# Two attention stages: cross attention's head order and output unit, local attention's scores, minimum and products

## The chip, the cores and the metric

The kernel runs on one core of one Trainium2 chip. The metric is the device time of one launch in microseconds (us). TensorE (PE) multiplies, VectorE (DVE) and ScalarE (ACT) do the elementwise work and empty PSUM, SyncE (SP) issues the weight loads. The engines run their own instruction streams in order and meet through semaphores.

## The reference

Two blocks of a small language model follow each other, 512 tokens wide 1024, all in float32. The first has two layers of mixer, memory cross attention and gated MLP; the second a gated linear attention layer and a local attention layer, each with an MLP. The two parts that matter here:

```python
def memory_cross_attention(x, mem_n, w_q, w_k, w_v, w_o):     # twice; 4 heads of 256, 256 memory rows
    s = einsum('bshd,bmhd->bhsm', q, k) * (256 ** -0.5)
    p = softmax(s, axis=-1)
    o = einsum('bhsm,bmhd->bshd', p, v).reshape(B, S, D_MODEL)
    return o @ w_o
```

The local attention (once) has 16 query heads of 64, two key heads, blocks of 128 queries that see their own and the previous block, a relative position bias with a mask in it, and one learned sink logit for each head, which enters the softmax's maximum and sum but has no value:

```
s = q k / 8 + bias[h];   m = max(max_k s, sink[h]);   p = exp(s - m) / (sum_k exp(s - m) + exp(sink[h] - m));   o = p v
```

## The kernel before

Activations lie with features on the partitions: `xs` is 8 tiles of 128 features by 512 tokens. A weight matrix comes in units of 128 x 2048 numbers. SP loads a unit into one of two raw buffers, ACT rounds it into `w_hi` (`split_hi`, L1206), DVE subtracts to get `w_lo` (`split_lo`, L1704), and a product with it is three matmuls (`mm3`: high by high, high by low, low by high), so that a unit of 256 output features is 8 tiles x 2 halves x 3 = 48 matmuls of 512 columns. The activations are split the same way (`high` on ACT, `rest` on DVE, into `xh` and `xl`). The products inside attention (queries by keys, transposes, probabilities by values) are plain float32, and PE runs each as two instructions.

All of PE's results go to eight PSUM banks. `plan_banks` (L120) lists the fills of every bank in PE's order; `wait_full`, `wait_free` and `wait_drained` wait for a fill, for the bank to be empty before a fill, and for the fill to have been read out. The order of work is the order written in each engine's program; there is no scheduler.

Cross attention is a pipeline of steps over the four heads. In step h PE computes the scores of head h (`s`), the output `o` of head h-2, and transposes the probabilities of head h-1 (`pT`). ACT takes the exponentials of head h straight from PSUM with a row sum, DVE finds the row maximum (L2048) before that and multiplies by the reciprocal of the sum afterwards (L2041, signal `p_ready`); both engines share the copies of `pT`; ACT and DVE split the output of a head into `xh` and `xl`. `queries_ahead` weaves the first two steps between the four query units: unit 0, unit 1, step 0, unit 2, step 1, unit 3, steps 2 to 5. On DVE the call before step 1 is `split_lo` of the output unit 0, which waits for ACT's half of that unit (`w_hi`), and ACT can't make that before query unit 2 is used up. After step 5 PE runs the four output units `xo`; unit 0 waits tile by tile for the heads' outputs.

Local attention (`swa`) runs 16 items, each a pair of heads (j = 0, 1, in partitions 0 to 63 and 64 to 127 of a query tile) by half of the sequence (nn: two blocks, n = 0, 1). In step `it` PE computes the scores of item `it`, half a half unit of the next queries (12 matmuls, up to step 11), the outputs of item it-2 and the transposes of item it-1; in the last steps it takes tiles of the output unit `so` in between. Scores of head j contract 64 rows; outputs of head j go to 64 columns of the array, that is to partitions 64j to 64j+63 of one bank. DVE adds the bias while reading PSUM (L2338, L2339, L2344), reduces the sum to the row maximum (L2341, L2342, L2347), takes the maximum with the sink and negates it (L2349, signal `rowmax_ready`); ACT takes the exponentials in place (L1665); DVE normalises (L2328, `p_ready`); PE transposes (L1158); ACT drains the transposes into `spT`. The even items (nn = 0) have three quarters of the columns, as the first block has no previous one. On ACT the drains of item it-2 stand ahead of the exponentials of item it, and behind those of item it-1.

Of the kernel before, what the change touches and what calls it, by code (L numbers as in the profile page):

```python
# [24 lines left out]
ACT = mybir.ActivationFunctionType  # L25
# [94 lines left out]
def plan_banks():  # L120
# [133 lines left out]
    for l in range(2):  # L254
# [8 lines left out]
        pairs(f"xo{l}", 4)  # L263
# [123 lines left out]
def build(nc, x, mem, params, consts, table, w_gk2, sinks, w, out):  # L387
    scratch = nc.dram_tensor("rel_scratch", [16, 384], F32, kind="Internal").ap()
    with ExitStack() as ctx:
# [41 lines left out]
        sb(ctx, "row_pad", [P, 120])  # L431
# [204 lines left out]
        def _(pe):  # L636
# [217 lines left out]

            def cross_attention(l):
# [3 lines left out]
                def step(h):  # L859
# [11 lines left out]
                    if h >= 2:  # L871
                        g = h - 2
                        if l == 1 and g == 0:
                            wait_drained(pe, ("mv1b", 1, 1))
                        for mt in range(MT):
                            wait_drained(pe, (name, "pT", g, mt))
# [129 lines left out]
            for l in range(2):  # L1006
# [3 lines left out]
                for j in range(4):  # L1010
                    feature_unit(f"xo{l}", j, ready=(lambda k: wait_drained(pe, (f"xa{l}", "o", k // 2, k % 2))) if j == 0 else None)
# [96 lines left out]
            def swa(it):  # L1108
# [4 lines left out]
                if it < SWA_ITEMS:  # L1113
                    hp, nn = it // 2, it % 2
                    if nn == 0:
                        wait_drained(pe, ("sq", hp // 2, hp % 2))
                    for j in range(2):
                        key = ("swa", "s", it, j)
                        wait_free(pe, key)
                        r = slice(64 * j, 64 * j + 64)  # L1120
                        for n in range(2):
                            blk = 2 * nn + n
                            lo = max(blk - 1, 0) * P
                            wd = (blk + 1) * P - lo
                            last = mm(bank(key)[:, (n + 1) * 256 - wd:(n + 1) * 256], qv[r, hp, blk * P:(blk + 1) * P],
                                      kk[r, hp // 4, lo:lo + wd], True, True)
                        full(last, key)
                if it in SWA_QUERIES:
                    half_unit("sq", 1 + it // 4, it // 2 % 2, range(4 * (it % 2), 4 * (it % 2) + 4), xtile)
                if it >= 2:  # L1130
# [5 lines left out]
                    for j in range(2):  # L1136
                        wait_drained(pe, ("swa", "pT", g, j))
                        for n in range(2):
                            blk = 2 * nn + n
# [53 lines left out]
        def _(act):  # L1193
# [435 lines left out]
            def drain_bias(m):  # L1629
                key = ("bias", m)  # L1630
                drain(key, bias[:, 2 * m:2 * m + 2, :], bank(key)[:, :].rearrange("p (h k) -> p h k", h=2))
# [20 lines left out]
            def swa(it):  # L1652
# [5 lines left out]
                if it < SWA_ITEMS:  # L1658
                    hp, nn = it // 2, it % 2
                    for j in range(2):  # L1660
                        seen.next("rowmax_ready")
                        for n in range(2):
                            lo = P if 2 * nn + n == 0 else 0
                            s_ = mh[:, it % 2, j, n * 256 + lo:(n + 1) * 256]
                            act.activation(s_, s_, ACT.Exp, bias=rmax[:, it % 2, 2 * j + n:2 * j + n + 1],  # L1665
# [24 lines left out]
        def _(dve):  # L1690
# [325 lines left out]
            def queries_ahead(split, drain_unit, step, steps):  # L2016
                for j in range(4):
                    split(j)
                    if j >= 2:
                        step(j - 2)  # L2020
                    drain_unit(j)
                for s in range(2, steps):
                    step(s)

            def cross_attention(l):
                name = f"xa{l}"

                def step(h):
# [4 lines left out]
                    if 1 <= h <= HEADS:  # L2033
# [8 lines left out]
                        give(last, "p_ready")  # L2042
                    if h < HEADS:
# [263 lines left out]
            def scaled_queries(j, m):  # L2307
                key = ("sq", j, m)
                wait_full(dve, key)
                free(dve.scalar_tensor_tensor(qv[:, 2 * j + m, :], bank(key)[:, :], 0.125, rstd[:, :], ALU.mult, ALU.mult), key)  # L2310
# [159 lines left out]
```

## Time and profile before

| | us |
|---|---|
| median of 3 runs | 2598.83 (2593.54 to 2599.11) |
| the profiled execution | 2598.96 |
| its span, first to last instruction | 2597.2 |
| PE busy in the span | 2488.3 (96%) |
| DVE busy | 1504.2 (58%) |
| ACT busy | 881.0 (34%) |

All times below are in us from the start of the span. Cross attention of layer 0 lies at about 330 to 402, of layer 1 at about 920 to 993; local attention runs from 2089 to 2190. 1.8 us of the profiled execution's time lie outside its span.

### The profile page before, as it was taken

What the parts mean: (1) busy time and instruction counts of PE and PEld (TensorE: products, weight loads), DVE (VectorE), ACT (ScalarE), POOL (GpSimd) and SP (SyncE); (2) the same over time, 40 slices, a digit from 0 to 9 for tenths busy, and PEclk for the clock granted to TensorE, in tenths of its full rate; (3) what the DMA queues carried; (4) which work ended last, traced back from release to release, by engine and by line L of the source; (5) the groups of instructions that cost most, each with busy time, mean ns of one, the idle gap of its engine ahead of it and who ended that gap; (6) DMA issues with size and microseconds to landing.
All of it is one profiled execution on the core that took longest, in us unless ns stands there. A gap on an engine that the chain in (4) does not pass through costs nothing.

```text
span 2597.2 us, 29768 instructions
## 1 busy us (share of the span) xinstructions
PE 2488.3 (96%) x11776; PEld 2036.6 (78%) x11776; DVE 1504.2 (58%) x2043; ACT 881.0 (34%) x1184; POOL 9.9 (0%) x23
## 2 busy tenths in 40 slices
PE   8999999999999799999998999999999998999998
PEld 7898777788887577788886788778888777788886
DVE  6887634644446834644446535556666686566666
ACT  3444533422223543422224434322222455322222
POOL 0000000000000000000000000000000000000000
PEclk9998999999999799999999999999999999999999
DMA  5222211322222121222222220132222211222221
GB/s 187 81 82 85 94 65 65 103 95 96 96 97 94 53 79 65 77 95 95 95 96 82 81 98 33 67 116 96 96 97 97 81 49 49 81 97 97 97 97 65
DMA packets 32816, 225.56 MB, mean 87 GB/s; under 512 B 3766, under 2 KB 3814, under 8 KB 6369
## 3 DMA queue, kind: packets, MB, share of 16 engines
q1 hardware_dynamic: 31536, 220.21, 24.7%
q0 software_dynamic: 1200, 4.23, 0.4%
q8 instruction: 57, 0.93, 0.1%
q14 instruction: 23, 0.18, 0.0%
HBM read 222.30 MB, written 2.12 MB: 86 GB/s over the span
## 4 chain that ended last, share of the span: by engine, by line
PE 83%; DVE 10%; ACT 4%; issue 2%; DMA 0%; DVEq 0%; SPq 0%; ACTq 0%
PE bank L640 83%; DVE w_lo L1708 2%; ACT w_hi L1207 1%; ACT xs L1266 1%; DVE xs L1791 1%; ACT xh L1220 1%; DVE cacc L1899 1%; DVE hs L1950 0%; DVE xs L1805 0%; DVE xs L1760 0%; DVE xl L1716 0%; DVE gs L1950 0%; DVE mh L2328 0%; DVE rmax L2347 0%; DVE mh L2344 0%
## 5 line engine op out<-in xcount | busy, mean ns | idle before, releaser
L640 PE MATMUL bank<-xh,w_hi 128*128 128x512 f32 x1976 | 789.7, 400 | 59.1 <-DVE xl L1716 22.0
L640 PE MATMUL bank<-xl,w_hi 128*128 128x512 f32 x1976 | 779.3, 394 | 0.0
L640 PE MATMUL bank<-xh,w_lo 128*128 128x512 f32 x1976 | 778.3, 394 | 0.0
L1708 DVE TENSOR_TENSOR w_lo<-w_raw,w_hi 128x2048 fp32r<-128x2048 f32 x205 | 469.6, 2291 | 410.3 <-ACT w_hi L1207 409.8
L1207 ACT ACTIVATE w_hi<-w_raw 128x2048 fp32r<-128x2048 f32 x205 | 391.2, 1909 | 373.2 <-PE bank L640 373.1
L640 PEld LDWEIGHTS bank<-xh,w_hi 128*128 128x128 f32 x1976 | 377.0, 191 | 158.9 <-issue 36.6
L640 PEld LDWEIGHTS bank<-xh,w_lo 128*128 128x128 f32 x1976 | 377.0, 191 | 80.2
L640 PEld LDWEIGHTS bank<-xl,w_hi 128*128 128x128 f32 x1976 | 377.4, 191 | 79.2 <-issue 2.2
L1760 DVE TENSOR_TENSOR xs<-xs,bank 128x512 f32<-128x512 f32 x448 | 294.2, 683 | 116.6 <-PE bank L640 115.4
L640 PE MATMUL bank<-mhh,w_lo 128*128 128x512 f32 x512 | 199.2, 389 | 0.0
L640 PE MATMUL bank<-mhh,w_hi 128*128 128x512 f32 x512 | 199.2, 389 | 0.0
L640 PE MATMUL bank<-mhl,w_hi 128*128 128x512 f32 x512 | 199.2, 389 | 0.0
L1851 DVE TENSOR_TENSOR mh<-bank,rstd 128x512 f32<-128x512 f32 x64 | 43.9, 692 | 178.6 <-PE bank L640 178.6
L1331 ACT ACTIVATE mhh<-mh 128x512 fp32r<-128x512 f32 x64 | 39.5, 633 | 317.3 <-DVE mh L1856 317.3
L640 PE MATMUL bank<-fhh,w_hi 128*128 128x512 f32 x352 | 136.9, 389 | 0.0
L640 PE MATMUL bank<-fhl,w_hi 128*128 128x512 f32 x352 | 136.9, 389 | 0.0
L640 PE MATMUL bank<-fhh,w_lo 128*128 128x512 f32 x352 | 136.9, 389 | 0.0
L1226 ACT ACTIVATE sq<-xs 128x512 f32<-128x512 f32 x88 | 54.7, 630 | 185.3 <-DVE xs L1760 69.4
L640 PEld LDWEIGHTS bank<-mhl,w_hi 128*128 128x128 f32 x512 | 96.1, 188 | 20.1
L640 PEld LDWEIGHTS bank<-mhh,w_hi 128*128 128x128 f32 x512 | 96.1, 188 | 19.9
L640 PEld LDWEIGHTS bank<-mhh,w_lo 128*128 128x128 f32 x512 | 96.1, 188 | 19.8
L1849 DVE TENSOR_TENSOR fh<-sil,bank 128x512 f32<-128x512 f32 x44 | 30.0, 687 | 116.6 <-PE bank L640 109.5
(286 smaller groups left out, 2719.9 us busy)
## 6 DMA issues: line engine op xcount, KB each, us to landing
w_raw<-weights_in SPq DMA_DIRECT2D x205, 1024.0 KB, 4.9
xs<-x_in SPq DMA_DIRECT2D x4, 512.0 KB, 8.0
sf<-rel_scratch POOLq DMA_DIRECT2D x1, 2048.0 KB, 11.8
y_out<-xs SPq DMA_DIRECT2D x8, 256.0 KB, 2.0
w_raw<-weights_in SPq DMA_DIRECT2D x2, 512.0 KB, 6.8
mk<-mem_in POOLq DMA_DIRECT2D x1, 1024.0 KB, 8.7
sum_q<-consts_in POOLq DMA_DIRECT2D x1, 256.0 KB, 8.9
scan<-consts_in POOLq DMA_DIRECT2D x1, 256.0 KB, 2.9
```

Of the source, the lines that this page charges most:

```text
L640: return pe.matmul(dst, a, b, start=start, stop=stop)
L1207: act.activation(w_hi[:, c % 2, :], w_raw[:, c % 2, :], ACT.Copy).then_inc(w_hi_ready, 1)
L1220: give(act.activation((xh if dst is None else dst)[:, k, :], src, ACT.Copy, **kw), "x_hi")
L1226: give(act.activation(sq[:, k % 2, :], src, ACT.Square), "sq_ready")
L1266: give(act.activation(xs[:, k, :], xs[:, k, :], ACT.Identity, scale=col(f"{param}_g{l}", k), bias=col(f"{param}_b{l}", k)), "xn_ready")
L1331: give(act.activation(hh[:, chunk % 2, m, :], src, ACT.Copy), "hh_ready")
L1708: dve.tensor_tensor(w_lo[:, c % 2, :], w_raw[:, c % 2, :], w_hi[:, c % 2, :].bitcast(F32), ALU.subtract)\
L1760: free(dve.tensor_tensor(xs[:, k, :], xs[:, k, :], bank(key)[:, :], ALU.add), key)
L1791: centred[k] = steps.step(dve.tensor_tensor(x_at(k), x_at(k), mean[:, :], ALU.subtract))
L1849: free(dve.tensor_tensor(hid[:, m, :], sil[:, m, :], bank(key)[:, :], ALU.mult), key)
L1851: free(dve.tensor_tensor(hid[:, chunk % 2, m, :], bank(key)[:, :], rstd[:, :], ALU.mult), key)
L1899: ins = dve.scalar_tensor_tensor(a, u, wj, a, ALU.mult, ALU.add)
```

## The change

In the plan of banks and on PE, the output unit 0 of cross attention moves to banks 4 and 5, which the scores have left, and its tiles are issued in pairs: tiles 0 and 1 in step 4 ahead of the outputs of head 2, tiles 2 and 3 in step 5 ahead of the outputs of head 3, tiles 4 to 7 after step 5.

```diff
         queries_ahead(f"xq{l}", cross(f"xa{l}"), HEADS + 2)
-        pairs(f"xo{l}", 4)
+        fill((f"xo{l}", 0, 0), 4)
+        fill((f"xo{l}", 0, 1), 5, UNITS[f"xo{l}"])
+        for j in range(1, 4):
+            pair(f"xo{l}", j)
...
+            def out_tiles(l, tiles):
+
+                stage = f"xo{l}"
+                c = UNITS[stage]
+                if tiles[0] == 0:
+                    pe.wait_ge(w_lo_ready, c + 1)
+                    for m in range(2):
+                        wait_free(pe, (stage, 0, m))
+                for k in tiles:
+                    wait_drained(pe, (f"xa{l}", "o", k // 2, k % 2))
+                    for m in range(2):
+                        last = mm3(bank((stage, 0, m))[:, :], weights(c, k * 256 + m * P, P), xtile(k), k == 0, k == KT - 1)
+                        if k == KT - 1:
+                            full(last, (stage, 0, m))
...
                         g = h - 2
                         if l == 1 and g == 0:
                             wait_drained(pe, ("mv1b", 1, 1))
+                        if h >= HEADS:
+                            out_tiles(l, range(2 * (h - HEADS), 2 * (h - HEADS) + 2))
...
                 queries_ahead(f"xq{l}", cross_attention(l), HEADS + 2, tile_ready)
-                for j in range(4):
-                    feature_unit(f"xo{l}", j, ready=(lambda k: wait_drained(pe, (f"xa{l}", "o", k // 2, k % 2))) if j == 0 else None)
+                out_tiles(l, range(4, KT))
+                for j in range(1, 4):
+                    feature_unit(f"xo{l}", j)
```

On DVE the normalisation of head 0 in step 1 moves ahead of the split of the output unit 0; the split of query unit 3 stays at the head of step 0.

```diff
-                def step(h):
+                def step(h, unit=None):
...
                         give(last, "p_ready")
+                    if unit is not None:
+                        split_lo(unit)
                     if h < HEADS:
...
-                queries_ahead(lambda j: j and split_lo(UNITS[f"xq{l}"] + j + 1), lambda j: None, cross_attention(l), HEADS + 3)
+                step = cross_attention(l)
+                split_lo(UNITS[f"xq{l}"] + 2)
+                for h in range(HEADS + 3):
+                    step(h, UNITS[f"xq{l}"] + 3 + h if h < 2 else None)
```

In local attention the score is kept negated: queries are scaled by -0.125, the bias is drained with scale -1, the sinks are negated once into `nskb`, and one DVE instruction for each block adds the bias and reduces to the minimum, seeded with the negated sink. It replaces the additions, the reductions and the small instruction behind them. ACT's exponential gets scale -1, and waits for the bank to be drained in place of `rowmax_ready`.

```diff
+            steps.step(dve.tensor_scalar(nskb[:, :], skb[:, :], -1.0, None, ALU.mult))
+            steps.wait()
...
-                        s_ = mh[:, it % 2, j, :]
-                        m_ = rmax[:, it % 2, 2 * j:2 * j + 2]
                         wait_full(dve, key)
-                        if nn == 0:
-                            dve.tensor_tensor(s_[:, P:2 * P], bank(key)[:, P:2 * P], bias[:, h, P:2 * P], ALU.add)
-                            free(dve.tensor_tensor(s_[:, 2 * P:], bank(key)[:, 2 * P:], bias[:, h, :], ALU.add), key)
-                            wait_drained(dve, key)
-                            dve.reduce_max(m_[:, 0:1], s_[:, P:2 * P], AX.X)
-                            steps.step(dve.reduce_max(m_[:, 1:2], s_[:, 2 * P:], AX.X))
-                        else:
-                            free(dve.tensor_tensor(s_.rearrange("p (n k) -> p n k", n=2), bank(key)[:, :].rearrange("p (n k) -> p n k", n=2),
-                                                   bias[:, h, :].unsqueeze(1).broadcast_to([P, 2, 2 * P]), ALU.add), key)
-                            wait_drained(dve, key)
-                            steps.step(dve.reduce_max(m_, s_.rearrange("p (n k) -> p n k", n=2), AX.X))
-                        steps.wait()
-                        give(dve.tensor_scalar(m_, m_, skb[:, h:h + 1], -1.0, ALU.max, ALU.mult), "rowmax_ready")
+                        for n in range(2):
+                            lo = P if 2 * nn + n == 0 else 0
+                            a = slice(n * 256 + lo, (n + 1) * 256)
+                            last = dve.tensor_tensor_reduce(mh[:, it % 2, j, a], bank(key)[:, a], bias[:, h, lo:], 1.0, nskb[:, h:h + 1],
+                                                            ALU.add, ALU.min, rmax[:, it % 2, 2 * j + n:2 * j + n + 1])
+                        free(last, key)
```

On PE the loops over heads and blocks are exchanged: both heads' banks (scores) or both heads' drained transposes (outputs) are waited for first, and then the products of the two heads alternate.

```diff
                     for j in range(2):
                         wait_drained(pe, ("swa", "pT", g, j))
-                        for n in range(2):
-                            blk = 2 * nn + n
-                            for kt in range(2):
-                                if blk + kt == 0:
-                                    continue
-                                v = (blk - 1 + kt) * P + (hp // 4) * 64
+                    for n in range(2):
+                        blk = 2 * nn + n
+                        for kt in range(2):
+                            if blk + kt == 0:
+                                continue
+                            v = (blk - 1 + kt) * P + (hp // 4) * 64
+                            for j in range(2):
                                 last = mm(bank(key)[64 * j:64 * j + 64, blk * P:(blk + 1) * P], vt[:, v:v + 64],
```

## Rows read from the trace of the kernel before

**Rows 1.** The page, part 1: engine, busy us, share, instructions.

```profile
PE 2488.3 (96%) x11776; PEld 2036.6 (78%) x11776; DVE 1504.2 (58%) x2043; ACT 881.0 (34%) x1184; POOL 9.9 (0%) x23
```

**Rows 2.** PE's waits, 357 to 413 (layer 0): total us, times, longest.

```profile
PE bank L891 <- DVE pr L2041: 2.6, 1, 2.6
PE bank L640 <- ACT pT L1212: 1.7, 2, 0.8
```

**Rows 3.** Timeline of PE, layer 1: start, length, [idle before].

```profile
953.51 1.38 PE L891 MATMUL bank<-ident,pr 128*128 128x128 f32 x8 [2.62 <-DVE pr L2041]
```

**Rows 4.** Stretch of steps 0 to 11: length, busy of each engine, PE clock.

```profile
2088.60:2160.00 71.40, 70.11 (x459) 53.13 (x460) 66.91 (x203) 45.37 (x148) 0.00 (x0) 1.00 0.13 45
```

**Rows 5.** Waits of PE 2088.6 to 2160; of PE, then ACT, 2160 to 2190.

```profile
PE bank L640 <- DVE sf L2310: 1.1, 2, 0.6
...
PE bank L640 <- ACT spT L1212: 6.1, 4, 2.9
...
ACT mh L1665 <- DVE rmax L2349: 7.3, 8, 1.8
```

**Rows 6.** Two stretches of low clock; the columns as in rows 4.

```profile
363.75:367.16 3.41, 3.41 (x13) 3.02 (x12) 2.03 (x6) 1.93 (x8) 0.00 (x0) 0.51 0.69 274
...
2183.05:2186.47 3.42, 3.42 (x19) 2.99 (x15) 2.00 (x2) 2.48 (x3) 0.00 (x0) 0.51 0.00 0
```

**Rows 7.** Timelines of ACT, DVE and PE around step 1, layer 0.

```profile
351.00 0.21 ACT L1442 ACTIVATION_READ_ACCUMULATOR pr<-bank,rmax 128x1 f32 x1
...
359.89 2.29 DVE L1708 TENSOR_TENSOR w_lo<-w_raw,w_hi 128x2048 fp32r<-128x2048 f32 x1 [10.65 <-ACT w_hi L1207]
...
362.31 1.14 DVE L2041 TENSOR_SCALAR pr<-pr,rinv 128x256 f32<-128x256 f32 x4
...
357.04 0.39 PE L640 MATMUL bank<-xh,w_lo 128*128 128x512 f32 x1
357.27 3.61 PE L640 MATMUL bank<-mk,qf 128*128 128x256 f32 x16
...
363.50 1.85 PE L891 MATMUL bank<-ident,pr 128*128 128x128 f32 x8 [2.62 <-DVE pr L2041]
```

**Rows 8.** Timelines of PE and DVE, steps 4 and 5 of layer 0.

```profile
397.01 1.04 PE L891 MATMUL bank<-ident,pr 128*128 128x128 f32 x8
398.88 3.67 PE L640 MATMUL bank<-pT,mv 128*128 128x512 f32 x8 [0.83 <-ACT pT L1212]
...
394.58 1.28 DVE L1716 TENSOR_TENSOR xl<-bank,xh 128x512 fp32r<-128x512 f32 x2
...
405.02 2.29 DVE L1708 TENSOR_TENSOR w_lo<-w_raw,w_hi 128x2048 fp32r<-128x2048 f32 x1 [1.04 <-ACT w_hi L1207]
```

**Rows 9.** PE timeline, steps 2 and 3; then instants: matmuls under way (x).

```profile
2107.93 1.58 PE L640 MATMUL bank<-spT,vt 128*64 128x128 f32 x16
...
2101.81 1.14 PE L640 MATMUL bank<-spT,vt 128*64 128x128 f32 x12
2102.89 1.09 PE L1158 MATMUL bank<-ident,mh 128*128 128x128 f32 x8
...
2108.84:2108.86 0.02, 0.02 (x5) 1.00 0.00 0
...
2093.40:2093.42 0.02, 0.02 (x4) 1.00 0.00 0
```

**Rows 10.** DVE groups by form: busy us, mean ns; the last two lie elsewhere.

```profile
L2347 DVE TENSOR_REDUCE rmax<-mh 128x2 f32<-128x512 f32 x16 | 11.0, 686 | 0.6
L2344 DVE TENSOR_TENSOR mh<-bank,bias 128x512 f32<-128x512 f32 x16 | 11.0, 685 | 0.1
...
L2349 DVE TENSOR_SCALAR rmax<-rmax,skb 128x2 f32<-128x2 f32 x32 | 7.3, 229 | 1.1
...
L1950 DVE SCALAR_TENSOR_TENSOR gs<-gs,hdec,bank 128x256 f32<-128x256 f32 x24 | 11.5, 481 | 0.9
...
L2152 DVE TENSOR_TENSOR_SCAN hb<-sum_q,hb 128x512 f32<-128x512 f32 x4 | 4.5, 1191 | 0.0
```

More of the change, by code:

```diff
@@ L430, in build @@
         invpos = sb(ctx, "invpos", [P, PAD])
-        sb(ctx, "row_pad", [P, 120])
+        nskb = sb(ctx, "nskb", [P, 16])
+        sb(ctx, "row_pad", [P, 104])
         w_raw = sb(ctx, "w_raw", [P, 2, UNIT])
@@ L1116, in swa @@
                         wait_drained(pe, ("sq", hp // 2, hp % 2))
+                    keys_ = [("swa", "s", it, j) for j in range(2)]
                     for j in range(2):
-                        key = ("swa", "s", it, j)
-                        wait_free(pe, key)
-                        r = slice(64 * j, 64 * j + 64)
-                        for n in range(2):
-                            blk = 2 * nn + n
-                            lo = max(blk - 1, 0) * P
-                            wd = (blk + 1) * P - lo
-                            last = mm(bank(key)[:, (n + 1) * 256 - wd:(n + 1) * 256], qv[r, hp, blk * P:(blk + 1) * P],
+                        wait_free(pe, keys_[j])
+                    for n in range(2):
+                        blk = 2 * nn + n
+                        lo = max(blk - 1, 0) * P
+                        wd = (blk + 1) * P - lo
+                        for j in range(2):
+                            r = slice(64 * j, 64 * j + 64)
+                            last = mm(bank(keys_[j])[:, (n + 1) * 256 - wd:(n + 1) * 256], qv[r, hp, blk * P:(blk + 1) * P],
                                       kk[r, hp // 4, lo:lo + wd], True, True)
-                        full(last, key)
+                            if n == 1:
+                                full(last, keys_[j])
                 if it in SWA_QUERIES:
@@ L1137, in swa @@
                         wait_drained(pe, ("swa", "pT", g, j))
-                        for n in range(2):
-                            blk = 2 * nn + n
-                            for kt in range(2):
-                                if blk + kt == 0:
-                                    continue
-                                v = (blk - 1 + kt) * P + (hp // 4) * 64
+                    for n in range(2):
+                        blk = 2 * nn + n
+                        for kt in range(2):
+                            if blk + kt == 0:
+                                continue
+                            v = (blk - 1 + kt) * P + (hp // 4) * 64
+                            for j in range(2):
                                 last = mm(bank(key)[64 * j:64 * j + 64, blk * P:(blk + 1) * P], vt[:, v:v + 64],
@@ L1630, in drain_bias @@
                 key = ("bias", m)
-                drain(key, bias[:, 2 * m:2 * m + 2, :], bank(key)[:, :].rearrange("p (h k) -> p h k", h=2))
+                drain(key, bias[:, 2 * m:2 * m + 2, :], bank(key)[:, :].rearrange("p (h k) -> p h k", h=2), scale=-1.0)
             drain_bias(0)
@@ L1660, in swa @@
                     for j in range(2):
-                        seen.next("rowmax_ready")
+                        wait_drained(act, ("swa", "s", it, j))
                         for n in range(2):
@@ L1664, in swa @@
                             s_ = mh[:, it % 2, j, n * 256 + lo:(n + 1) * 256]
-                            act.activation(s_, s_, ACT.Exp, bias=rmax[:, it % 2, 2 * j + n:2 * j + n + 1],
+                            act.activation(s_, s_, ACT.Exp, scale=-1.0, bias=rmax[:, it % 2, 2 * j + n:2 * j + n + 1],
                                            accum_out=rsum[:, it % 2, 2 * j + n:2 * j + n + 1])
@@ L2014, in linear_attention @@
                 outputs(HEADS - 1)
[L2016 to L2023, printed above, removed]
             def cross_attention(l):
                 name = f"xa{l}"
-                def step(h):
+                def step(h, unit=None):
                     if 2 <= h < HEADS + 2:
@@ L2309, in scaled_queries @@
                 wait_full(dve, key)
-                free(dve.scalar_tensor_tensor(qv[:, 2 * j + m, :], bank(key)[:, :], 0.125, rstd[:, :], ALU.mult, ALU.mult), key)
+                free(dve.scalar_tensor_tensor(qv[:, 2 * j + m, :], bank(key)[:, :], -0.125, rstd[:, :], ALU.mult, ALU.mult), key)
             dve.wait_ge(sinks_loaded, 16)
+            steps.step(dve.tensor_scalar(nskb[:, :], skb[:, :], -1.0, None, ALU.mult))
+            steps.wait()
             for m in range(8):
@@ L2333, in swa @@
                         key, h = ("swa", "s", it, j), 2 * hp + j
[L2334 to L2335 removed]
                         wait_full(dve, key)
[L2337 to L2349 removed]
+                        for n in range(2):
+                            lo = P if 2 * nn + n == 0 else 0
[3 more added lines that the diff above has]
+                        free(last, key)
                 if it in SWA_QUERIES and it % 2:
```

## The prediction, made before the changed kernel was run

> **What bounds the kernel.** I read the page first: PE is busy 96% of the span [rows 1], so only idle time of PE, time at low clock, or PE's own work can give anything. Then PE's waits in the three places that the diff touches. In cross attention PE stands still three times in each layer: 2.62 us before the transposes of head 0, for DVE's normalised probabilities, and twice 0.83 us before the outputs of heads 2 and 3, for ACT's copy of the transposes [rows 2, 3]. In local attention steps 0 to 11 are dense on PE (70.1 of 71.4 us), but DVE is busy 66.9 of those 71.4, so it is nearly the bound itself [rows 4]; PE waits for it twice there, 1.1 us in all. In the last steps, without query work in between, PE waits 6.1 us for ACT's drains, once 2.9 us, and ACT in turn 7.3 us for DVE's maxima [rows 5]. Last the clock: after the 2.6 us of idleness, and after the 2.9 us, PE ran at 0.51, the level of 1.2 GHz, for 3.4 us, and then at 2.4 GHz again [rows 6]. Half of such a stretch is lost where PE is the bound: 3.4 x 0.49 = 1.7 us; I take 1.6.
>
> **Cross attention, normalisation ahead of the split.** ACT has all exponentials and sums of head 0 at 351.2. DVE normalises only at 362.31 because `split_lo` of output unit 0 stands in front and waits 10.65 us for `w_hi`, then takes 2.29 us [rows 7]. Moved ahead, the normalisation is done near 353, in DVE time that was idle. PE ends its scores at 357.27 + 3.61 = 360.88 and found nothing to do until 363.50; it would go on at once: 2.6 us, and about 0.1 us of overlap between neighbours, so 2.7. The split itself can't start before 359.89 in either order, so it ends at 362.2 as before; what follows on DVE (reciprocal and four products, 1.3 us) is gone, so head 1's maxima start 1.2 us earlier. Nothing of query unit 3 hangs on this split: its own `w_lo` was made in step 0, and SP's weight loads stay tied to the same splits. Without the gap the stretch of low clock should go too: 1.6 us. Layer 1 has the same wait of 2.62 us [rows 3]. Bounds: 2.6 if the clock falls anyway, 4.4 if both go. I take 4.3.
>
> **Cross attention, tiles between heads.** From the transposes of head 3 to its outputs PE takes 398.88 - 397.01 = 1.87 us, where the transposes alone need 1.04 less some 0.15 of overlap: 1.0 us is idle, and the same before head 2. Twelve matmuls at 0.23 us each (357.04 to 357.27) [rows 7] make 2.7 us of work, far more than the wait. They are no new work, only moved: 24 of the 48 are issued earlier. Do their own waits hold? Tiles 2 and 3 need DVE's halves of head 1, done at 394.58 + 1.28 [rows 8], and would start near 400; tiles 0 and 1 need head 0, one step earlier still; banks 4 and 5 are empty once the exponentials of head 3 are read, before head 2's transposes. Behind these matmuls stand the outputs of heads 2 and 3, which so start up to 2 us later than without them; ACT and DVE have slack. Next to be late: the `w_lo` of output unit 1, ready at 405.02 + 2.29 = 407.31, which is 4.8 us behind the end of head 3's outputs (398.88 + 3.67) [rows 8]; before, 48 matmuls (10.9 us) covered it, now 24 (5.4 us). The margin is 0.6 us; if it fails, it costs up to 0.5. I take 0.95 for each wait, 1.9 a layer, between 1.2 and 2.0.
>
> Cross attention together: 2 x (4.3 + 1.9) = 12.4 us.
>
> **Local attention, alternating heads.** Outputs: sixteen matmuls of an odd item last 1.58 us, twelve of an even one 1.14, and eight transposes, one after another, 1.09 [rows 9], thus 0.11 us from start to start. Near the end of the odd item's row five matmuls are under way at one instant: two column halves run beside each other. But sixteen in strict sequence would take 15 x 0.11 + 0.27 = 1.9 us and in perfect pairs 1.09; 1.58 says that the second head starts when some three products of the first are left. Alternating should reach the pairs: 0.49 us for odd items. For twelve, 1.14 against 5 x 0.11 + 0.05 + 0.27 = 0.87: 0.27. Scores: four matmuls of 256 columns are under way at one instant, where each lasts about 0.38 and could be followed after 0.21: the two heads are already paired (four a head seems to be few enough). I give this edit nothing. The waits for both heads' banks or drains in front cost nothing in the dense part. Of the sixteen outputs ten lie there: 5 x (0.49 + 0.27) = 3.8 us, between 0 and 4.
>
> In a sentence apart: the Trainium skill (TensorE: Matmul & The Clock Gate, Back-to-back issue gap) puts a sustained stream of weight load and matmul at 128 columns at about 81 ns apart; sixteen would then take 15 x 0.081 + 0.27 = 1.5 us whatever the order, and the edit would bring under 0.1 us an item. The trace's instant with five under way, each of 0.27 us, is one every 54 ns, but over less than half a microsecond. This is rival B.
>
> **Local attention, the fused instruction.** A head of an odd item costs DVE an addition (0.69), a reduction (0.69) and the small one (0.23), about 1.57 with their overlap [rows 10]; an even one 1.44. After: two fused instructions. The trace has none. The nearest row is a three-operand instruction of 256 columns with a per-partition scalar, one operand in PSUM: 0.481. Below, nothing excludes the plain rate, 0.33 each with overlap; above, the scan, which is serial, has 1.19 for 512 columns, so some 0.65 for 256. With up to 0.15 for writing the result out, a head costs 0.7 to 1.6; I take 1.1, 0.95 for even items. That frees DVE about 1 us an item. In steps 0 to 11 PE's two waits for DVE go, 1.1 us, and DVE stays clear of the period that alternation shortens from 5.95 to 5.5. Signs, the one instruction for the sinks and ACT's scale cost nothing: DVE stood idle there and the ACT instructions keep their shapes.
>
> In steps 12 to 17 each of three long waits ends with ACT's drains, which stand behind two exponentials, which wait for DVE. The first head's minimum comes 0.47 earlier and the gap before the second (0.3) closes: 0.75 less. The outputs then wait for both drains instead of one (0.5 later) and last 0.49 less, which cancels. I take 0.65 for each of the three, 1.95, and 0.27 for the alternation of item 14, which PE's path holds. With the long wait down from 2.9 to some 2.2 us the low clock behind it [rows 6] may or may not stay: 0.8 of 1.6. Tail: 3.0, between 0.5 and 4.5.
>
> Local attention: 3.8 + 1.1 + 3.0 = 7.9 us.
>
> **Sum.** 12.4 + 7.9 = 20.3 us off the profiled execution's 2598.96, of which the span is 2597.2 and the rest stays: 2578.7 us. The profiled execution stands at the median of the runs, 2598.83, so no shift. The chip's stretches of low clock at other places may come out differently by one or two, 1.6 us each; the fastest run before (2593.54) shows as much. The forecast's own range is 2574 to 2584.
>
> **Rivals.**
> A. The fused instruction runs at the scan's rate: 1.6 us a head, DVE not relieved. For it: it carries a value from column to column, as the scan does; against it: the reductions do as well and cost 0.69 for 512. PE could then gain from alternation only until DVE is full (66.9 of 71.4 us, in part overlap): 1.5 us, and 0.3 in the tail. 2598.96 - 12.4 - 1.8 = 2584.8. The Trainium skill (Vector Engine (DVE) Microarchitecture Reference, Points that are easy to get wrong) says that an instruction with accumulator and two wide SBUF sources halves its rate; here one source is in PSUM, and no row shows either.
> B. The alternation brings nothing, because issue sets the pace: 2598.96 - 20.3 + 3.8 + 0.3 = 2582.8. Against it stands the instant with five under way.
> C. Slower than before: the fused instruction, of a kind that no row has, carries a large fixed price. DVE's other work is 66.9/12 - 2 x 1.6 = 2.4 us an item, so an item takes 2.4 + 4c and sixteen of them replace 101.4 us; with cross attention's 12.4 the point of no gain is c = (113.8/16 - 2.4)/4 = 1.18 us, 2.5 times the nearest row. At c = 1.3 the time would be 2598.96 + 121.6 - 101.4 - 12.4 = 2606.8. Nothing in the profile speaks for it.
> D. The waits only move and the whole is within 0.2%: the transposes of head 0 meet another wait, and local attention stays tied to its chain.
>
> **How the numbers follow.** Forecast 0.74, A 0.09, B 0.10, C 0.05, D 0.02. Faster by over 0.2%, about what a measurement of this kernel can tell, are the first three: 0.93; same 0.02; slower 0.05. The range must hold the forecast with its clock stretches, B, and A's time: 2571 to 2588.
>
> **What would show it.** Cross attention: no wait of PE for L2041's successor, clock 1.0 through query unit 3, that unit's start near 361.8, outputs of heads 2 and 3 without a wait, each layer 6 us shorter. If PE waits for `w_lo` before output unit 1, the margin was misjudged. Local attention: outputs' rows near 1.1 and 0.87 us; fused instructions of 0.4 to 0.55 us; DVE near 55 us busy where it had 66.9; the step from the queries' last product to the first of `so` unit 0's second half some 8 us shorter. Fused instructions of 0.65 and more mean A or C; outputs at 1.5 mean B.

## The result, and the profile after

The changed kernel takes 2575.34 us (median of 4 runs, 2573.81 to 2575.63); the kernel before, in the same comparison, 2597.45 (2593.54 to 2599.11). The ratio is 0.9916, 95% interval 0.9901 to 0.9931. The forecast was 2578.7, a gain of 20.3 us; the medians say 22.1. The kernel before, measured again beside each group of experiments, has medians of 2595.61 to 2597.39, so up to 1.8 us of those 22.1 may be scatter. The profiled execution took 2575.22 us with a span of 2573.4, 23.8 us under the span before.

I read the page's PE line first (busy us, share, instructions), against [rows 1]:

```profile
PE 2477.0 (96%) x11776; PEld 2028.1 (79%) x11776; DVE 1482.1 (58%) x2044; ACT 879.1 (34%) x1184; POOL 9.9 (0%) x23
```

The same matmuls take 11.3 us less busy time, some of it low clock and some the outputs that now run in pairs; the rest of the 23.8 us was idleness. Then layer 0 of cross attention, where [rows 7, 8] were. Timelines of DVE and PE (start, length, instruction, [idle before]):

```profile
351.32 1.14 DVE L2057 TENSOR_SCALAR pr<-pr,rinv 128x256 f32<-128x256 f32 x4
...
403.82 2.29 DVE L1733 TENSOR_TENSOR w_lo<-w_raw,w_hi 128x2048 fp32r<-128x2048 f32 x1 [1.04 <-ACT w_hi L1232]
...
357.13 3.61 PE L644 MATMUL bank<-mk,qf 128*128 128x256 f32 x16
360.58 1.04 PE L912 MATMUL bank<-ident,pr 128*128 128x128 f32 x8
...
397.75 3.59 PE L644 MATMUL bank<-pT,mv 128*128 128x512 f32 x8
```

Head 0 is normalised at 351.3 in place of 362.3, its transposes follow the scores at 360.58 with no idleness, the outputs of head 3 start without the 0.83 us in brackets, and between 357 and 413 no wait of PE is left where [rows 2] had 4.3 us. The clock of the 50 us from the scores of head 1 to output unit 0 is full, where [rows 6] had 3.4 us at 0.51 (columns as in [rows 4]; the second and third line are local attention, steps 0 to 11 and the steps behind):

```profile
357.00:407.00 50.00, 50.00 (x212) 36.93 (x211) 21.22 (x40) 18.07 (x43) 0.00 (x0) 1.00 0.06 21
...
2074.00:2142.00 68.00, 67.85 (x469) 50.46 (x469) 53.20 (x207) 45.59 (x150) 0.00 (x0) 1.00 0.15 50
2142.00:2166.00 24.00, 18.95 (x170) 13.91 (x167) 18.35 (x71) 17.30 (x55) 0.00 (x0) 1.00 0.02 2
```

In the second line DVE is busy 53.2 us of 68 where it had 66.9 of 71.4 [rows 4]; the prediction said near 55. (The line opens 1.7 us before the first score of item 0; from there to the first score of step 12 DVE is busy 52 of 66 us.) Of PE's waits of [rows 5], those for DVE's `sf` are gone; the waits for ACT's drains, and ACT's for DVE, in 2142 to 2170 are (us in all, times, longest):

```profile
PE bank L644 <- ACT spT L1237: 4.7, 4, 1.9
...
ACT mh L1690 <- DVE rmax L2361: 4.8, 4, 2.0
```

PE's 6.1 us became 4.7, and no stretch of low clock follows the longest. The outputs, against [rows 9], and the fused instruction with its read of the accumulator, which [rows 10] could only bound (groups by form over 2074 to 2166: busy us, mean ns; then two in the order of time):

```profile
2133.84 0.88 PE L644 MATMUL bank<-spT,vt 128*64 128x128 f32 x12
...
2146.61 1.09 PE L644 MATMUL bank<-spT,vt 128*64 128x128 f32 x16 [1.28 <-ACT spT L1237]
...
L2361 DVE CUSTOM_DVE_ANT_0 mh<-bank,bias,nskb 128x256 f32<-128x256 f32 x48 | 21.3, 480 | 3.7 <-PE bank L644 3.7
...
L2361 DVE DVE_READ_ACCUMULATOR2_ANT rmax<- 128x1 f32 x64 | 5.3, 84 | 0.0
...
2137.29 0.48 DVE L2361 CUSTOM_DVE_ANT_0 mh<-bank,bias,nskb 128x256 f32<-128x256 f32 x1
2137.70 0.09 DVE L2361 DVE_READ_ACCUMULATOR2_ANT rmax<- 128x1 f32 x1
2137.70 0.48 DVE L2361 CUSTOM_DVE_ANT_0 mh<-bank,bias,nskb 128x256 f32<-128x256 f32 x1
```

One instruction lasts 0.48 us, just what the nearest row of before had, but the next one starts 0.41 us after it, beside the accumulator's read: a head costs 0.81 us, not 1.1, and an even item's head 0.68, not 0.95.

To separate what each edit does from the stretches of low clock elsewhere, which come out differently from kernel to kernel, I measured three stretches in every trace, each between the starts of the same two matmuls: cross attention of each layer (first score of head 0 to the last tile of output unit 3) and local attention with its output projection (first score of item 0 to the last tile of unit 3). They are differences of two start times of one trace; less than before is a gain.

```
us                   cross 0  cross 1  local    median, kernel / before of that comparison
before                102.34   102.32  139.25
changed                95.81    95.81  128.74   2575.34 / 2597.45
cross_norm             97.87    97.88  139.25   2590.24 / 2595.92
cross_tiles           100.25    98.64  139.23   2593.26 / 2595.92
local_alt             102.25   102.30  141.33   2597.44 / 2595.92
local_fused           102.33   100.71  132.63   2588.81 / 2595.92
after_seq_outputs      95.81    95.81  132.54   2579.39 / 2595.61
cross_busy            100.70   100.72  139.21   2595.04 / 2595.61
dve_alternates         95.81    95.81  129.58   2575.70 / 2595.61
fused_twice            95.81    95.81  140.77   2586.71 / 2595.61
outputs_by_block       95.81    95.81  130.65   2577.16 / 2597.39
tail_tiles             95.81    95.81  128.02   2575.36 / 2597.39
tail_act               95.81    95.81  129.31   2574.48 / 2597.39
tail_filled            95.81    95.81  125.14   2569.53 / 2595.65
```

Where two kernels have the same code in a stretch, and low clock falls into it equally, their traces agree within 0.04 us but for local_alt's cross attention (0.1); a stretch of low clock more or less shifts one by about 1.6 us. The medians scatter far more. One of the twelve executions of cross_norm took 9536.8 us, at a granted clock of 0.416; the ratio below leaves it out.

Local attention has two parts that behave differently, so here is its time once more, cut at the first score of step 12: steps 0 to 11, in which PE has query work, and all that follows, called the last steps below.

```
us                   steps 0 to 11   last steps
before                    70.92        68.33
changed                   65.83        62.91
local_alt                 68.65        72.68
local_fused               69.68        62.95
after_seq_outputs         69.63        62.91
outputs_by_block          66.33        64.32
fused_twice               68.28        72.49
```

Cross attention gained 6.53 + 6.51 = 13.0 us (forecast 12.4), local attention 10.5 (forecast 7.9). Together they are 23.5 of the span's 23.8.

### The profile page after: what moved, and what is told of

Same layout as the page of the kernel before. It is cut to its first block, busy times and chain, and to the rows that moved or that the text cites. A ratio compares the mean times of both kernels' runs of the same rounds, so it can differ in the third digit from the quotient of the medians.

```text
span 2573.4 us, 29864 instructions
## 1 busy us (share of the span) xinstructions
PE 2477.0 (96%) x11776; PEld 2028.1 (79%) x11776; DVE 1482.1 (58%) x2044; ACT 879.1 (34%) x1184; POOL 9.9 (0%) x23
## 4 chain that ended last, share of the span: by engine, by line
PE 86%; DVE 8%; ACT 4%; issue 1%; DMA 0%; DVEq 0%; SPq 0%; ACTq 0%
PE bank L644 85%; DVE w_lo L1733 2%; ACT w_hi L1232 1%; ACT xs L1291 1%; DVE xs L1816 1%; DVE cacc L1924 1%; ACT xh L1245 1%; DVE hs L1975 0%; DVE xs L1830 0%; PE bank L1183 0%; DVE xs L1785 0%; DVE xl L1741 0%; DVE gs L1975 0%; PE bank L912 0%; DVE sum_x L1752 0%
```

## The experiments

### Cross attention, each edit alone

**cross_norm**: before, with DVE's scaling of head h-1 ahead of the split.

```
-            queries_ahead(lambda j: j and split_lo(...+ j + 1), lambda j: None, cross_attention(l), HEADS + 3)
+                    if unit is not None:        # in step(h), behind the scaling
+                        split_lo(unit)
```

> The kernel before, with only this changed: in cross attention DVE scales the finished head's probabilities ahead of the split of an output unit. My theory: the wait of 2.6 us before the transposes of head 0 goes and with it the stretch of low clock behind it, 2.7 + 1.6 = 4.3 us a layer; the trace of the changed kernel showed about 4.5. So 8.6 to 9.0 us off, with no low clock in query unit 3. First rival: the low clock does not come from this wait and stays, then 2 x 2.7 = 5.4 us off. Second rival: the wait only moves to another place, 0 to 2 us off.

The ratio is 0.9979 (0.9969 to 0.999), 5.7 us in medians. By the stretches: 4.47 and 4.44 us. The whole term of 4.3 is there, and both rivals are out. The waits left between 330 and 420, which the kernel before has too:

```profile
PE bank L640 <- ACT pT L1212: 1.7, 2, 0.8
PE bank L640 <- DVE w_lo L1708: 0.5, 1, 0.5
```

**cross_tiles**: before, with `out_tiles` ahead of the outputs of heads 2 and 3.

```
+                        if h >= HEADS:
+                            out_tiles(l, range(2 * (h - HEADS), 2 * (h - HEADS) + 2))
```

> The kernel before, with only this changed: in cross attention two times two tiles of output unit 0 are issued ahead of the outputs of heads 2 and 3. My theory: it fills twice 0.95 to 1.05 us of idleness a layer, 3.8 to 4.2 us off in all, and the wait of 2.6 us with its low clock stays. With the normalisation still behind the split, the low half of output unit 1 comes later relative to PE by nothing that matters. Rival: the tiles only move idleness to the wait for the low half of output unit 1 or to the outputs of head 3, 0 to 1.5 us off.

The ratio is 0.9989 (0.9981 to 0.9998). Layer 0 is 2.09 us shorter, as expected. Layer 1 is 3.68 us shorter, which neither theory had: it has the same wait of 2.62 us, and yet the clock did not fall. The transposes behind the wait in both layers, and the 3.4 us that follow (PE clock is the number behind POOL):

```profile
360.96 1.50 PE L911 MATMUL bank<-ident,pr 128*128 128x128 f32 x8 [2.62 <-DVE pr L2062]
...
949.22 1.09 PE L911 MATMUL bank<-ident,pr 128*128 128x128 f32 x8 [2.62 <-DVE pr L2062]
...
361.10:364.50 3.40, 3.40 (x14) 2.91 (x14) 2.04 (x5) 1.93 (x8) 0.00 (x0) 0.56 0.69 277
949.20:952.60 3.40, 3.38 (x19) 2.97 (x20) 1.96 (x5) 1.93 (x8) 0.00 (x0) 1.00 0.77 292
```

The transposes' 1.50 against 1.09 us is how a low clock looks in a timeline. Without that stretch of 1.6, layer 1's own gain is 2.07 again. The two edits add up: 4.46 + 2.07 = 6.53.

### Whether idleness lowers the clock

**cross_busy**: before, with more PE work in the wait.

```
-                            for t in range(2):
+                            for t in (0, 1, 0, 1) if (h, g) == (1, 1) else (0, 1):
```

> The kernel before, with four score matmuls of head 1 in each cross attention done twice (0.45 us each, 1.8 us of PE work a layer that leaves the result as it is), in the 2.6 us in which PE otherwise waits for the probabilities of head 0. My theory: the low clock behind the wait comes from PE's idleness. With a wait of 0.8 us in place of 2.6 the clock stays at 1.00 and each layer is 1.6 us shorter although PE does more: 3.3 us off. Rival: the low clock follows from something else (the weight stream, the time since the last one, the work before); then it stays at 0.51 in query unit 3 and the time is as before.

Each layer is 1.64 and 1.60 us shorter although PE executes 1.8 us more; the wait is 0.9 us and the clock of the stretch is full:

```profile
PE bank L891 <- DVE pr L2041: 0.9, 1, 0.9
...
357.00:407.00 50.00, 47.44 (x198) 34.25 (x197) 21.60 (x43) 15.76 (x40) 0.00 (x0) 1.00 0.11 38
```

The stretch came out as the theory says, and was worth 1.6 us. Two layers alone could be chance, because the low clock does not come each time: over before, cross_tiles, local_alt and local_fused, which all keep the wait of 2.62 us in both layers, the clock fell 6 times of 8 (local_fused, layer 1, is the other one that kept it; 100.71 against 102.33). Without that wait it never fell there: in none of the two layers of cross_norm, the two of cross_busy, and the sixteen of the changed kernel and the seven built on it. So the low clock goes with PE's idleness; what decides the two exceptions isn't shown. In the medians this kernel is the same as before (0.9997, 0.9987 to 1.0008): 3.2 us less in two places is lost in the scatter of the runs before (2590.39 to 2601.76), and only the stretches show it.

### Local attention, each edit alone

**local_alt**: before, with both loop orders of the change (the head `j` innermost) and DVE's old instructions.

> The kernel before, with only this changed: in local attention the two heads alternate in the scores and the outputs, DVE works as before. Theory of the prediction's first rival, which is mine for this kernel: the rows of the outputs shrink from 1.58 to 1.09 us and from 1.14 to 0.88, but DVE is busy 66.9 of 71.4 us there and each item of it hangs on the one before, so PE gets new waits for it: 0 to 1.8 us off. Rival: DVE had enough slack, and the edit alone brings its 3.8 us in steps 0 to 11.

A miss on the low side: 2.1 us longer, not 0 to 1.8 shorter (ratio 1.0005, 0.9995 to 1.0014). The rows of the outputs are 1.09 and 0.88 us as expected. PE's waits from 2088 to 2190, against 6.1, 1.1 and 0.6 before, and the two stretches of low clock (PE clock is the number behind POOL):

```profile
PE bank L640 <- ACT spT L1215: 8.1, 5, 2.7
PE bank L640 <- DVE sf L2313: 2.4, 3, 1.0
PE bank L640 <- DVE yl L1719: 0.6, 1, 0.6
...
2159.50:2166.40 6.90, 6.22 (x36) 4.70 (x35) 6.51 (x21) 4.59 (x18) 0.00 (x0) 0.51 0.01 4
2176.60:2186.90 10.30, 8.20 (x42) 6.33 (x43) 6.54 (x15) 6.79 (x16) 0.00 (x0) 0.50 0.08 12
...
2163.04 1.98 PE L640 MATMUL bank<-spT,vt 128*64 128x128 f32 x16 [0.68 <-ACT spT L1215]
...
2181.26 1.55 PE L640 MATMUL bank<-spT,vt 128*64 128x128 f32 x12 [2.10 <-ACT spT L1215]
```

The two parts go opposite ways. In steps 0 to 11 the edit gains 2.27 of its 3.8 us even beside the old DVE instructions, and the rest comes back as waits for DVE (1.1 us became 2.4). In the last steps it loses 4.35 us: the waits for both heads' drains grow (6.1 us became 7.9 there), waits of 2.7, 2.4 and 2.1 us come up, and some 17 us run at half clock, where before it was 3.4. Both rows of outputs shown are stretched by that.

**local_fused**: before, with `tensor_tensor_reduce`, the negated signs and ACT's `scale=-1.0`, PE's order as before.

> The kernel before, with only this changed: in local attention one fused instruction adds the bias and takes the row minimum, PE's order as before. My theory: PE's two waits for DVE go (1.1 to 1.3 us), and the tail's three waits shrink, the low clock with them: 4 to 5 us, so 5 to 6.5 us off. Rival: without the alternation the outputs wait for one head's drain only and start sooner, and the tail gives more, up to 7 us. Second rival: the gain of the tail belongs to the alternation, and this kernel gives 1 to 3 us.

6.62 us shorter in local attention, just above my 5 to 6.5; the ratio is 0.9969 (0.9958 to 0.998). Steps 0 to 11, same columns as [rows 4]:

```profile
2088.87:2158.55 69.68, 69.68 (x457) 52.91 (x457) 52.55 (x206) 45.52 (x149) 0.00 (x0) 1.00 0.14 46
```

PE waits for no other engine there, which is worth 1.24 us, and no low clock follows the waits of the last steps, which are 5.38 us shorter. They are as long as in the changed kernel (62.95 and 62.91 us), so neither rival holds: without the alternation they give no more, and their gain does not belong to it.

**after_seq_outputs**: the changed kernel with the outputs head by head again, the scores still alternating.

> The changed kernel, but its outputs in local attention run one head after the other as before; the scores still alternate. My theory: the fused instruction alone gained 6.6 us between the start and the end of local attention, both together 10.5, and the alternation of the scores is worth nothing; so the outputs' order is worth 3.9 us here, 3.8 of it in steps 0 to 11, and this kernel is 3.9 us slower than the changed one, about 18 us faster than before. Rival: part of the 3.9 us belongs to the scores, then only 2 to 3 us slower.

Local attention is 3.80 us longer than in the changed kernel; the medians, of two comparisons, are 4.1 apart. It is also within 0.1 us of local_fused, from which it differs in local attention by the scores' order alone: that edit is worth nothing. PE's waits in the last steps:

```profile
PE bank L644 <- ACT spT L1236: 2.5, 3, 1.6
PE bank L644 <- DVE yl L1740: 0.6, 1, 0.6
```

The six outputs there are 2.3 us longer than in the changed kernel, and PE waits 2.2 us less: in the last steps, 62.91 us in both kernels, alternation brings nothing, and all of its 3.8 us lies in steps 0 to 11.

**outputs_by_block**: the changed kernel with `for j` outside `for kt`, so turns of two matmuls.

> The changed kernel, but the heads alternate in the outputs of local attention every two matmuls (one block) instead of every one. In the trace of before, eight matmuls of one head stood in a row, and the second head's started when some three of the first were left. My theory: PE looks about four matmuls ahead for one that goes to the free column half, so turns of two are as good as turns of one: sixteen outputs in 1.09 us, twelve in 0.88, and the time of the changed kernel. Rival: only neighbours pair, the rows last some 1.3 to 1.6 us, and local attention is 2 to 4 us longer than in the changed kernel.

```profile
2115.19 1.15 PE L644 MATMUL bank<-spT,vt 128*64 128x128 f32 x16
```

Sixteen in 1.15 us, twelve in 0.93: 0.05 more each, near to turns of one and far from 1.58. Local attention was 1.9 us longer all the same. Ten rows at 0.05 make 0.5 of it in steps 0 to 11; in the last steps a stretch at low clock, which the changed kernel did not have, follows a wait of 1.91 us. The changed kernel has a wait of 1.93 and tail_tiles (below) one of 1.94 at the same place and no such stretch, so that this part comes from the edit is not shown:

```profile
2159.50:2162.90 3.40, 3.32 (x23) 2.95 (x23) 1.98 (x2) 2.93 (x3) 0.00 (x0) 0.67 0.00 0
```

### How much DVE work local attention stands

**fused_twice**: the changed kernel with each fused instruction issued twice, the copy into tiles that nobody reads.

> The changed kernel with each fused instruction of local attention issued twice, the second copy into a place that nobody reads. That adds 1.6 us of DVE work to an odd item and 1.4 to an even one. My theory: in steps 0 to 11 DVE's 53.2 us become about 71 of 68, so it is the bound again: 3 to 5 us there; and in the last steps the chain through DVE and ACT gets 0.8 us an item longer, 3 us and perhaps a stretch of low clock: 6 to 10 us slower than the changed kernel. First rival: DVE has slack everywhere, 0 to 2 us. Second rival: local attention hangs on DVE item by item throughout, 16 x 1.5 = 24 us slower.

12.0 us longer, more than my 6 to 10; the medians of two comparisons are 11.4 apart. Steps 0 to 11 gave 2.45 of it, less than my 3 to 5, and DVE's work there came out at 65.66 us, not 71. The last steps gave 9.6:

```profile
PE bank L645 <- ACT spT L1238: 7.9, 4, 2.5
PE bank L645 <- DVE sf L2332: 1.7, 3, 0.6
...
2078.50:2146.80 68.30, 66.00 (x457) 49.09 (x458) 65.66 (x290) 43.60 (x140) 0.00 (x0) 1.00 0.14 47
...
2151.80:2158.60 6.80, 6.19 (x35) 4.66 (x34) 6.59 (x34) 4.50 (x17) 0.00 (x0) 0.50 0.01 4
2168.80:2179.10 10.30, 7.82 (x43) 5.95 (x42) 6.46 (x20) 6.79 (x16) 0.00 (x0) 0.50 0.09 14
```

The low clock lasted 17 us in two stretches, and that is what I had undersized. The last steps hang on the chain through DVE; in steps 0 to 11 even a DVE that is busy 96% of the time costs PE only those 2.45 us.

### What is left in the last steps

**dve_alternates**: the changed kernel with one loop over `j` in DVE's step: scale head j of the last item, then the fused instructions of head j of the next.

> The changed kernel, but DVE alternates between scaling head j of the last item and the fused instructions of head j of the next one, where it first scaled both heads. In the last steps of local attention ACT waits for the minimum of the next item's first head, which stands behind the scaling of the second head (0.9 us) on DVE. My theory: each of the odd items' minima comes some 1 us sooner there, two to four times, and PE's 4.7 us of waits shrink by 2 us: 2 us faster than the changed kernel. Rival: the second head's probabilities come 0.8 us later instead, its transposes wait, and the time stays within 0.5 us or gets worse.

0.84 us longer; the theory fell, the rival holds. PE has a new wait, for the second head's probabilities:

```profile
PE bank L644 <- ACT spT L1237: 4.3, 4, 1.7
PE bank L1183 <- DVE mh L2351: 0.8, 2, 0.4
```

**tail_act**: the changed kernel with ACT's copies between the exponentials.

```
+                        if j and it in BETWEEN:          # items 12, 14, 15
+                            drain_turned(it - 1)
```

> The changed kernel, with ACT copying the transposes of item 11, 13 and 14 out between the two heads' exponentials of the next item instead of behind both. My theory: the outputs that wait 1.28, 1.28 and 1.93 us for these copies start some 1.05 us sooner, the second head's exponentials come 1.05 us later and with them its transposes, whose cover is thin: 0.5 us a time, 1.5 us faster than the changed kernel. Rival: the second head's probabilities become the wait that ends last, and nothing is gained or up to 1 us lost.

0.57 us longer: PE's waits for the copies fall to 3.3 us, and 1.2 us for the second head's probabilities come instead. Again the rival.

**tail_tiles**: the changed kernel with output tiles in the waits.

```
+                if it in SO_EARLY:
+                    half_unit("so", 0, 0, SO_EARLY[it], ytile, head_ready)
...
-            SO_TILES = {SO_FIRST: range(0, 4), SO_FIRST + 2: range(4, 5), SO_FIRST + 3: range(5, 6), SO_FIRST + 4: range(6, 7)}
+            SO_EARLY = {SO_FIRST: range(0, 1), SO_FIRST + 2: range(4, 5), SO_FIRST + 3: range(5, 6)}
+            SO_TILES = {SO_FIRST: range(1, 4), SO_FIRST + 3: range(6, 7)}
```

> The changed kernel, with the tiles of the output projection that stand in the last steps of local attention placed in PE's waits for ACT's drains: one of the four of step 13 and those of steps 15 and 16 ahead of the outputs (where PE waits 1.28, 1.28 and 1.93 us), the one of step 17 between the transposes and outputs of item 15. My theory: a tile is 0.9 us of work; the first saves 0.9, the last one 0.9, the others go from one wait into another: 1.8 us faster than the changed kernel. Rival: each wait is part of a chain through DVE and ACT that starts at PE's scores and outputs, and the tile ahead of them delays it: 0 to 0.5 us.

0.72 us shorter, of 1.8. The rival gives up to 0.5, but for another reason than what the trace shows: the waits for ACT fell from 4.7 to 2.9 us as the theory has it, but the tile moved from step 17 had covered DVE's reading of the last outputs, whose bank the second half of output unit 0 needs:

```profile
PE bank L644 <- ACT spT L1240: 2.9, 4, 1.9
PE bank L644 <- DVE yl L1744: 1.5, 1, 1.5
```

**tail_filled**: the tiles of tail_tiles, and that cause taken away.

```
-    fill(("so", 0, 1), 1, UNITS["so"])
+    fill(("so", 0, 1), 7, UNITS["so"])
...
+                    if it == SO_FIRST + 3:
+                        half_unit("so", 0, 1, range(0, 2), ytile)
...
-            half_unit("so", 0, 1, range(0, 7), ytile)
+            half_unit("so", 0, 1, range(2, 7), ytile)
```

> The changed kernel with the tiles of tail_tiles, and the second half of output unit 0 in bank 7, which is empty from the scores of item 14 on, in place of bank 1, which holds the outputs of the last head pair until DVE has read them. So its tiles 0 and 1 can stand in the wait before the outputs of item 14 too, and the rest follows the outputs of item 15 without a wait. My theory: of the 5.3 us that PE waits in the last steps of the changed kernel (4.7 for ACT's drains, 0.6 for DVE) about 1 us stays: 4.3 us faster than the changed kernel, about 2571 us, and no stretch of low clock there. Rival: tail_tiles brought 0.7 of 1.8 us because each tile ahead of the outputs delays the chain through DVE and ACT; then this one brings 1 to 2 us.

```profile
PE bank L644 <- ACT spT L1242: 1.5, 4, 0.5
...
2142.00:2166.00 24.00, 22.51 (x173) 16.88 (x172) 16.96 (x63) 16.77 (x54) 0.00 (x0) 1.00 0.09 31
```

3.60 us shorter in local attention (5.3 us of waits became 1.5), not far from the theory's 4.3 and above the rival's 1 to 2; PE is busy 22.5 of 24 us where the changed kernel had 18.95. Its median is 2569.53 us (2569.15 to 2570.21), ratio to before 0.9901 (0.9884 to 0.9919). It was not run beside the changed kernel (0.9916, 0.9901 to 0.9931), so the comparison with that one rests on the traces: of the 5.2 us between the profiled spans (2568.2 and 2573.4) 1.6 come before local attention, where the two kernels issue the same work, so the edit's own worth is 3.6 us, not the medians' 5.8.

## Why the prediction was right

The time came out 3.4 us below the forecast, within its range, and the mechanisms were the forecast ones. The stretches gained 23.5 us where the sum had 20.3; 2.4 of the 3.2 between them are the last steps of local attention. By its own steps:

- **Normalisation ahead of the split, 4.3 a layer: 4.46.** Both halves are shown apart: cross_norm removed wait and low clock, cross_busy the low clock alone (1.62), so the wait is 2.84. I had subtracted nothing for the clock's uncertainty; that it fell in both layers of the trace before was luck with the trace, 6 layers of 8, not a rule.
- **Tiles between heads, 1.9 a layer: 2.07.** PE's outputs of heads 2 and 3 start without a wait, and the margin of 0.6 us held: the split ended at 403.82 + 2.29 = 406.11, and PE, which came to output unit 1 at 406.6, did not wait for it: 0.5 us.
- **Alternation of the outputs, 3.8 in steps 0 to 11: 3.8** (after_seq_outputs), once the fused instruction was there. Without it, 2.3 in the same steps (local_alt), and 4.35 lost in the last ones. Rival B is out. Rival A's argument, that a nearly full DVE leaves PE only a part of it, was sound in steps 0 to 11 (it had 1.5); its 0.3 for the last steps was wrong in sign. In a sentence apart: the Trainium skill (TensorE: Matmul & The Clock Gate, Back-to-back issue gap) has some 81 ns between such matmuls as the sustained rate; the changed kernel's row of sixteen has 1.09 - 0.27 = 0.82 us from the first start to the last, 55 ns apart, so that rate is no floor where two column halves take turns.
- **Scores, 0: 0.** local_fused and after_seq_outputs agree within 0.1 us.
- **DVE's two waits, 1.1: 1.3** (the gain of after_seq_outputs in steps 0 to 11).
- **The tail, 3.0: 5.4.** This is the term that was mis-sized. From [rows 5] to after_seq_outputs PE's waits fell from 6.1 to 2.5, 3.6 us, where I had 1.95. The first of the three long ones, before and in after_seq_outputs (PE, the outputs of item 11):

```profile
2165.69 1.58 PE L640 MATMUL bank<-spT,vt 128*64 128x128 f32 x16 [1.48 <-ACT spT L1212]
...
2152.17 1.58 PE L644 MATMUL bank<-spT,vt 128*64 128x128 f32 x16 [0.43 <-ACT spT L1236]
```

  The head costs 0.81 us, not 1.1, so the first minimum comes 0.76 us earlier and not 0.47. With the gap of 0.3 that closes as forecast this makes 1.06, and two of the three waits fell by 1.05 and 1.01, where I had taken 0.65. The third, the longest, fell by 1.31 (2.94 to 1.63), and a short one of 0.2 went. The low clock went altogether, 1.6 where I booked half; that is partly luck, because outputs_by_block has it behind a wait as long as the changed kernel's. The 0.27 for item 14's alternation did not show: the tail's shorter outputs all became waits.
- **The fused instruction's price.** I added up to 0.15 us to the nearest row for writing the result out; the trace shows the opposite, 0.07 us of overlap between neighbours. A and C are out, and so is D: the waits did not move elsewhere. The Trainium skill's page Vector Engine (DVE) Microarchitecture Reference (Points that are easy to get wrong) halves the rate with an accumulator and two wide SBUF sources; here one of them is in PSUM, and the row's 0.48 us is that of the three-operand instruction without accumulator in [rows 10], so nothing is halved.

## What to carry to other kernels

The alternation cost 2.1 us alone and brought 3.8 beside the fused instruction, and a sum over the whole stage hides why: it gained 2.3 us where PE had other work, although DVE was 94% busy there, and lost 4.35 where PE hung on the chain through DVE and ACT. So judge an edit part by part of a stage, and shorten the chain before you make PE wait for more of it. A stall shorter than a tile of independent work is best filled with such a tile, but ask first what the tile covered where it stood, and which bank it needs. And where a wait of a few microseconds ends, look at the clock behind it: it can cost more than half of the wait again.

## What the runs showed of the hardware

- The same wait of PE, 2.62 us, was followed by about 3.4 us at half clock 6 times of 8, at a cost of 1.6 us each, and a wait of 1.9 us once (outputs_by_block) and not in the changed kernel nor in tail_tiles; after waits of 0.8 and 0.9 us in cross attention it was not. In local_alt and fused_twice, with several waits of 2.1 to 2.7 us close together, stretches of 6.8 and 10.2 us followed.
- Matmuls that use 64 columns of the array, in alternating halves, start 55 ns apart over sixteen; in turns of two, nearly so (1.15 against 1.09 us); with eight of one head and then eight of the other, 87 ns (1.58).
- The fused add and row minimum on 256 columns, one operand in PSUM, takes 480 ns, its accumulator read 84 ns, and both overlap with the next, 0.41 us from start to start; 128 columns take 0.35 and 0.27.
